# A fused two-block fp32 layer stack: the two token halves of a projection tile, one after the other or chunk by chunk

## What is computed

```
h = rmsnorm(x); z = h @ w_in                       # then a gated recurrence (oa) and a band attention (ob)
merged = sigmoid(gate_a) * (oa @ w_branch_a) + sigmoid(gate_b) * (ob @ w_branch_b)      # merge
x = x + merged @ w_out                                                                  # wout
x = x + (silu(h2 @ w_ffn_gate) * (h2 @ w_ffn_up)) @ w_ffn_down                          # gu, dn0..dn2
x = x + sigmoid(h3 @ w_ple_gate) * (p @ w_ple_proj)                                     # proj, pleg
u = rmsnorm(x) @ w_in_a        # conv, gates, scan, then x = x + y @ w_out_a            # xg, wo1, wo2
ckr = rmsnorm(x) @ w_dkv; u = rmsnorm(x) @ w_in_b                                       # dkv, cq, cgate
x = x + attention_output @ w_out_b; out = rmsnorm(x)                                    # wob
```

## Time and profile before

| | us |
|---|---|
| three executions | 2645.43, 2646.66, 2649.67 |
| their median | 2646.66 |
| the profiled execution, its own time | 2644.31 |
| span of that execution, first to last instruction | 2642.2 |
| TensorE matmul busy in it | 2555.2 (97%) |
| VectorE busy | 1494.2 (57%) |
| GpSimd busy | 1074.3 (41%) |
| mean granted TensorE clock | 0.99 |

### The profile page before, as it was taken

How to read it: one execution, slowest core, us unless ns; L and a number is a source line. 1 busy time by engine, 2 the same in 40 slices (tenths; PEclk the granted TensorE clock), 3 DMA queues, 4 the chain that set the end, 5 groups by cost and what they waited for, 6 DMA issues and landing times.

```text
span 2642.2 us, 32837 instructions
## 1 busy us (share of the span) xinstructions
PE 2555.2 (97%) x12732; PEld 2127.0 (81%) x12732; DVE 1494.2 (57%) x1820; ACT 905.6 (34%) x1265; POOL 1074.3 (41%) x770
## 2 busy tenths in 40 slices
PE   7999999899999989999999999999999999999997
PEld 6888887787788778888888887788888787888876
DVE  4485633376655687677652254667774524555554
ACT  5244235322222343333330032345641422444432
POOL 3453522211233478888854343333355332111111
PEclk9999999999999999999999999999999999999999
DMA  3101021111252122222252122311132311000022
GB/s 132 48 25 41 33 80 40 48 37 45 99 190 70 40 74 86 80 88 80 88 183 96 63 65 72 107 40 44 43 119 80 114 64 30 20 20 17 25 81 78
DMA packets 52888, 184.01 MB, mean 70 GB/s; under 512 B 5409, under 2 KB 9761, under 8 KB 51361
## 3 DMA queue, kind: packets, MB, share of 16 engines
q1 hardware_dynamic: 46560, 147.08, 16.6%
q10 hardware_dynamic: 6208, 35.27, 3.5%
HBM read 149.83 MB, written 32.51 MB: 69 GB/s over the span
## 4 chain that ended last, share of the span: by engine, by line
PE 53%; DVE 6%; ACT 3%; issue 2%; POOL 0%; ACTq 0%; DVEq 0%; POOLq 0%
PE ps L784 10%; PE ps L786 10%; PE ps L785 10%; PE ps L1097 5%; PE ps L1099 5%; PE ps L1098 5%; PE ps L1277 2%; PE ps L1267 1%; PE ps L1195 1%; PE ps L1197 1%; PE ps L1196 1%; DVE tmp L2412 1%; PE ps L1256 0%; PE ps L1255 0%; PE ps L1254 0%
## 5 line engine op out<-in xcount | busy, mean ns | idle before, releaser
L584 POOL TENSOR_TENSOR derived_vectors<-w_staged 1x1 f32<-1x1 f32 x162 | 39.0, 241 | 1398.1 <-PE ps L786 683.9
L587 POOL TENSOR_TENSOR w_low<-w_staged,w_high 128x1024 fp32r<-128x1024 f32 x162 | 433.9, 2678 | 13.0
L848 PE MATMUL ps<-h_mix_high,w_high 128*128 128x512 f32 x688 | 279.6, 406 | 4.6 <-DVE z_hgrn_f L1913 4.6
L850 PE MATMUL ps<-h_mix_high,w_low 128*128 128x512 f32 x688 | 270.4, 393 | 0.0
L849 PE MATMUL ps<-h_mix_low,w_high 128*128 128x512 f32 x688 | 269.8, 392 | 0.0
L585 POOL CAST w_high<-w_staged 128x1024 fp32r<-128x1024 f32 x162 | 167.6, 1035 | 0.0
L848 PEld LDWEIGHTS ps<-h_mix_high,w_high 128*128 128x128 f32 x688 | 130.6, 190 | 30.8 <-issue 5.8
L850 PEld LDWEIGHTS ps<-h_mix_high,w_low 128*128 128x128 f32 x688 | 130.2, 189 | 28.3
L849 PEld LDWEIGHTS ps<-h_mix_low,w_high 128*128 128x128 f32 x688 | 130.7, 190 | 25.3
L784 PE MATMUL ps<-act_high,w_high 128*128 128x512 f32 x352 | 137.1, 390 | 0.7 <-DVE act_low L1850 0.7
L785 PE MATMUL ps<-act_low,w_high 128*128 128x512 f32 x352 | 137.0, 389 | 0.0
(11 more groups left out here) (511 smaller groups left out, 6927.6 us busy)
## 6 DMA issues: line engine op xcount, KB each, us to landing
w_staged<-weights_in SPq DMA_DIRECT2D x178, 512.0 KB, 3.5
w_staged_late<-weights_in SPq DMA_DIRECT2D x22, 512.0 KB, 4.3
gates_loaded<-gates ACTq DMA_DIRECT2D x8, 1024.0 KB, 6.5
gates<-tmp SPq DMA_DIRECT2D x16, 512.0 KB, 2.6
act_raw<-gates SPq DMA_DIRECT2D x16, 512.0 KB, 7.4
gates<-gates_staged_late SPq DMA_DIRECT2D x22, 256.0 KB, 2.0
x_in<-xT_in SPq DMA_DIRECT2D x8, 512.0 KB, 8.1
x_mid<-xT_in ACTq DMA_DIRECT2D x1, 4096.0 KB, 13.3
```

Of the source, the lines that this page charges most:

```text
L587: nc.gpsimd.tensor_tensor(w_low[:, j], w_staged[:, j], f32(w_high[:, j]), ALU.subtract).then_inc(s_split, 1)
L848: nc.tensor.matmul(ps[:, bank], wH, h1H[:, c, tok], start=(c == 0), stop=False)
L850: done = nc.tensor.matmul(ps[:, bank], wL, h1H[:, c, tok], start=False, stop=(c == DC - 1))
```

## The change

In `tile` the branch that alternates the halves is taken by every tile but the one with `between`. A tile with no `first_wait` waits for both banks at its start and then does chunk 0 of half 0, chunk 0 of half 1, chunk 1 of half 0, and so on. Of the tiles, the first of each stage with a `first_wait` and the last of wob stay as they were.

```
-                if first_wait:
+                if not between:
                     for h in range(2):
                         bank_read(h)
                     for n, (c, r) in enumerate(chunks):
-                        pe.wait_ge(*first_wait(r))
+                        if first_wait:
+                            pe.wait_ge(*first_wait(r))
                         for h in range(2):
                             chunk(h, n, c, r, low_chunk and low_chunk(r))
                 else:
...
                         bank_read(h)
                         for n, (c, r) in enumerate(chunks):
                             chunk(h, n, c, r, low_chunk and low_chunk(r))
-                            if between and h == 1 and n == 4:
+                            if h == 1 and n == 4:
                                 between()
```

## The result

| | before | changed |
|---|---|---|
| median of 20 executions each, us | 2648.15 | 2651.06 |
| lowest and highest, us | 2643.96, 2649.67 | 2648.26, 2653.82 |
| span of the profiled execution, us | 2642.2 | 2647.8 |
| ratio to before, 95% interval | | 1.0015 [1.0009, 1.0022] |

The changed kernel is slower by 0.15%, 4.0 us by the ratio (2.4 to 5.8), 2.9 by the medians. The forecast was +2.8 us, within 0.2%, 2649.5 with a range of 2645.5 to 2653.4.

A forecast was written before the change was run, and what follows sets the result against it. TensorE, busy 97% of the span, was taken to bound the kernel. Moved waits of 0.62 + 1.19 + 0.4 + 0.62 = 2.83, say +2.8 us, on the median 2646.66 gave 2649.5, range 2645.5 to 2653.4.

The forecast's parts named there:

- Pace inside a tile: Within a tile, alternating or sequential halves both take 10.88 us for 48 matmuls at PEclk 1.00: 0.
- When the halves are read: At tile ends, half 0 is read later, but reads still end 0.89 us after the tile: counted 0.
- The moved wait: At tile starts, TensorE waits for one read more: proj +0.62, wo1 +1.19, dkv +0.4, cgate +0.62 us.
- The sequel in wo1: GpSimd's subtraction ends 0.64 later, holding VectorE's L2429 and later reads: wo1 +1.19 us, without it 0.55.
- The sum: Over proj, wo1, dkv and cgate: 0.62 + 1.19 + 0.4 + 0.62 = 2.83, say +2.8 us.
- The bounds of the moved wait: Sum over the four places between 0 and 3.7 us; wo1 +0.1 to +1.8, proj and cgate at most 0.69 each.
- Profiled execution and median: Whole kernel: profiled execution 2644.31 us, median of three 2646.66; forecast set from the median, 2649.5.
- Costless waits: Rival: TensorE's restart or a later wait, for instance at xg's start, swallows the new waits; 2646.7 us, chance 0.08.
- Slower in xg: Rival: VectorE over 1.2 us later in xg stalls about nine blocks; +9.8 in all, 2656.5 us, chance 0.06.
- Slower by the clock: Rival: alternation idles TensorE between groups of three, lowering PEclk in changed tiles; +28, 2675 us, chance 0.03.

The follow-up runs named there:

- the alternation with the late wait: Changed kernel, but half 1's bank waited for only ahead of the first matmul that writes it; ratio to the kernel before 1.0000 [0.9991, 1.0009].
- The moved wait alone: Kernel before with its old order of halves, but both banks waited for at a tile's start; ratio to before 1.0014 [1.0005, 1.0023].
- the run with the third tile on time: Changed kernel, but wo1's third tile waits for half 1's bank only ahead of its first use; executed once, no ratio, wo1 cost 0.58 us.

## Why the prediction was right, point by point

- **Pace inside a tile, 0.** Right: 10.88 us for the tiles of 48 that do not begin behind a wait, PEclk 1.00, and a ratio of 1.0000 for the alternation with the late wait.
- **When the halves are read, 0.** Right: reads end 0.89 us after a tile's end in either order. The merged row ("x2") came as said; VectorE's idle time before it was 8.38 us in the tile shown, where "about 10" was named.
- **The moved wait.** Right in mechanism and in all four places: 0.64, 1.22, 0.41 and 0.65 against 0.62, 1.19, 0.4 and 0.62. The moved wait alone gave a ratio of 1.0014. The agreement to 0.03 is in part luck, since small errors cancel. A start follows the end of the second read by 0.15 us, where the end of the first read had been followed by 0.06 (the 0.10 of the prediction comes from cutting a merged row into equal parts), so the third tiles of proj, wo1 and cgate start 0.69 later and not 0.62 to 0.64, and the tile behind is 0.04 to 0.05 shorter than before. In dkv the start moved by 0.33 and not by 0.25, and the tile grew by 0.08 and not by 0.14.
- **The sequel in wo1.** Right: L2429 was held by GpSimd's later subtraction and took 2.50. The value without the sequel was put at 0.55, and the run with the third tile on time gave 0.58.
- **The sum.** 2.92 against 2.83. The measured loss is 4.0 by the ratio, with 2.4 to 5.8 in its interval, so the sum lies inside and no missing term is shown. One that may be missing is the clock in proj: 1.6 us in two of five profiles, on the average 0.6, which would make 3.6. The bounds of the moved wait, 0 to 3.7, left it out (the two profiles with the fall have 4.59 and 3.87 by place): I bounded the length of each stall and took TensorE's pace behind it as given. The upper ends that I wrote down, 0.69, 1.8, 0.4 and 0.69, add up to 3.6 and not 3.7; the range would be 0.1 shorter.
- **Profiled execution and median.** The executions of one kernel differ by more than the change. The untouched stages gave 2.7 of the 5.6 us between the two spans. Comparing the spans alone would have doubled the price. The forecast of 2649.5 was 1.6 below the measured 2651.06; 1.5 of it is the base, the median of three executions where that of twenty was 2648.15.
- **Rivals.** Costless waits: fallen, each delay is passed on. Slower in xg: fallen, 1.26 us of room as before. Slower by the clock: fallen in the form given, since alternating does not make TensorE idle, and from merge to cgate the stages that the change touches stand at 1.00 in all thirteen profiles, but for proj's third tile in two. What the rule of the Trainium skill that was named there ("TensorE: Matmul & The Clock Gate", "A second HAM failure mode: psum-queue depth-cycling") would bring, a clock that falls between the groups, no run here shows. A fall showed instead behind the stall that the moved wait made longer.

## What to carry to other kernels

When an order of work is changed, look at the waits that move with it: here the order was free and the wait, moved up by half a tile, was the whole price, while the same order with the wait at the first use cost nothing. The place to look is where the reader of a buffer is late already, and there the cure is to let the reader come earlier in its own program (or another engine read), which gained 0.14 to 0.20% against the kernel before in either order. Then look again: earlier reads let a tile start earlier, and the next late read can come to light. A delay of one engine can grow by way of a second and third, as the split on GpSimd shows, so follow it until it meets slack.

## What the runs showed of the hardware that was not expected

- The clock behind a stall is not the same in each execution. Behind 1.9 us of idle TensorE in proj it was at half speed for most of a tile in two of five profiles (4.41 us in place of 2.82). Behind 2.1 us in the feed-forward products PEclk was 1.00 in one profile of the kernel before and 0.66 in the other. What decides it no run here shows, and the chip is not ruled out.
- This is part of why the executions of one kernel differ by several us (2643.96 to 2649.67 before): 3.2 of the 4.6 us between the two profiles of the kernel before lie in two stretches, in stages that the change does not touch, where PEclk was 1.00 in one and 0.66 or 0.86 in the other.
- VectorE's L2429, which has two SBUF inputs and starts during GpSimd's subtraction, ends 1.08 or 1.09 us after it in thirteen profiles. A GpSimd that is 0.64 later moved VectorE's chain by as much.
- A price of 3 us can be read from starts of tiles, place by place, to 0.05 us, and from the total only with many executions.
